# Causal pooling by running sums on VectorE in place of pooling-matrix products, and layer-norm moments and scaling of the gating branch at hooks of their own

## The chip, the cores and the metric

The kernel runs on one core of a Trainium2 chip. The metric is the device time of one execution in microseconds. Each of the core's engines (TensorE, or PE; VectorE, or DVE; ScalarE, or ACT; GpSimd, or POOL; SyncE, or SP) has a queue of instructions that it works off in order; they wait for each other through semaphores.

## The reference

Two transformer-like blocks on 256 tokens of width 2048, in fp32. Two places matter here. The first block has a spatial gating unit, whose second half `v` goes through a layer norm over its 1024 channels before it is mixed along the tokens:

```python
vn = layer_norm(v, ln_g, ln_b)
mixed = einsum('gqp,bnpgc->bnqgc', w_s, vn.reshape(...)) + b_s
y = u * mixed
```

The second block begins with a pool mixer. Its 4096 channels `u` are four groups of 1024; in group j each token gets the mean of the last w tokens (w = 2, 4, 8, 16, fewer at the beginning), less itself:

```python
z = xn @ w_in;  u, g = split(z, 2)
for j, w in enumerate((2, 4, 8, 16)):
    c = csum[:, :, group j]            # running sum over tokens, a zero ahead
    count = minimum(t + 1, w)
    pooled_j = (c[:, 1:] - lagged by w) / count - u[:, :, group j]
mixed = einsum('bsgc,gcd->bsgd', pooled, w_group)
out = (mixed * scale * silu(g)) @ w_out
```

## The kernel before

Nearly all the work is products with weights that pass through the core once. SyncE loads them as 1 MB units into four raw tiles. So that fp32 accuracy is reached with the faster fp32r products, each unit is split in two halves: ScalarE rounds a half (`w_hi`, line 1438), VectorE subtracts (`w_lo`, line 2036, counted by `lo_split`), and TensorE makes three products for each pair of operands (lines 829 to 831, or 913 to 916 where the result is wanted with channels on partitions). There are four buffers of halves: ScalarE rounds half h only when TensorE has left half h - 4 (`act.wait_ge(half_used, h - 3)`).

The work is cut into stages (`STREAM`, line 79 on), a stage into rounds and chunks; a chunk is 512 result columns. `pool_u` has 4 rounds of 2 chunks of 8 halves. A round of `pool_g` has chunks of 4, 8, 4 and 8 halves: a product of the pooled channels with `w_group`, then a gate. `in_h` has 2 rounds of 2 chunks of 8 halves, with one sum of the conditioning (`add_ada`, line 2064) behind each four halves. All other work of ScalarE and VectorE is put by hand between the halves, at hooks: `run` calls a hook in the middle of each chunk, `run_at` at given numbers of halves. What a hook does stands on its engine's queue ahead of the rounding or subtraction of the next half.

Pooling, before: VectorE scales a finished chunk into `u_stage`, tokens on partitions (`pool_u_out`, line 2608). Behind the next chunk TensorE multiplies it with a pooling matrix over the tokens (`pool_turn`, line 1194: 4 x 3 fp32 products, `k_pool` loaded by GpSimd), so that the pooled channels come out on partitions in PSUM. ScalarE rounds them to `pooled_hi` (`direct`, line 1472), VectorE subtracts to `pooled_lo` (`pool_rest`, line 2599) and frees the PSUM tile (`fm_empty`).

Elsewhere, as behind each chunk of `m1a`, a tile is only turned: `turn` (line 922) makes 8 transposes into the same PSUM tiles.

The gating branch, before: in `in_h`, VectorE's hook of the second chunk does `conv_sides(0)` and then the moments of both token tiles (`sgu_norm`, line 2266); ScalarE's of the third takes the root; VectorE's of the fourth does `conv_sides(2)` and then scales both tiles (`sgu_norm2`, line 2272).

## Time and profile before

| | us |
|---|---|
| median of 3 runs | 2746.13 |
| lowest, highest | 2746.08, 2747.34 |
| the profiled execution | 2747.47 |
| its span, first to last instruction | 2746.1 |
| TensorE busy | 2662.0 (97%) |
| VectorE busy | 1812.8 (66%) |
| ScalarE busy | 1274.3 (46%) |
| mean granted TensorE clock | 0.985 |

Products overlap, so starts tell more than durations: the distance from the start of one product to that of a later one is what the stretch cost. A row in brackets at the end of a timeline line tells how long the engine had stood idle and what released it. PEclk 1.00 is the 2.4 GHz level, 0.50 the 1.2 GHz level.

### The profile page before, as it was taken

Reading aid. Unit: us, or ns where it says so; the run is one execution under the profiler, and the core shown is the slowest. Engines: PE = TensorE matmul, PEld = TensorE weight load, DVE = VectorE, ACT = ScalarE, POOL = GpSimd, SP = SyncE. Lnnn points to the kernel's source line nnn. Section 1 sums busy time; section 2 is a strip of 40 time slices with the busy share of each in tenths; the row PEclk is TensorE's granted clock in tenths of the full one; section 3 lists DMA queues with packets and bytes.
Section 4 is the critical chain, followed back from the end, with each engine's and each line's share of the span. In section 5 each row is a group of like instructions: output and inputs, shape, how many; then the busy total and the mean of one; then the engine's idle time right before and its main releaser. Section 6 shows DMA issues by size and latency. Waiting matters only on the chain.

```text
span 2746.1 us, 31839 instructions
## 1 busy us (share of the span) xinstructions
PE 2662.0 (97%) x12702; PEld 2213.7 (81%) x12702; DVE 1812.8 (66%) x1869; ACT 1274.3 (46%) x1544; POOL 36.1 (1%) x58
## 2 busy tenths in 40 slices
PE   4899999999999999999999899999999999999999
PEld 2569998888878888888888788888888888888887
DVE  6877878877897654578766855555555565656565
ACT  1234444334344444565555433444444565555463
POOL 0000000000000000000000000000000000000000
PEclk8899999999999999999999999999999999999999
DMA  9987677878868865566555555555565555533654
GB/s 320 335 305 271 227 278 260 280 268 318 305 223 309 278 217 188 188 202 198 189 198 191 195 173 173 175 184 184 184 210 195 184 185 175 184 123 123 214 184 138
DMA packets 269205, 599.47 MB, mean 218 GB/s; under 512 B 12739, under 2 KB 13390, under 8 KB 258638
## 3 DMA queue, kind: packets, MB, share of 16 engines
q1 hardware_dynamic: 259680, 561.56, 60.5%
q0 software_dynamic: 5472, 26.25, 2.8%
q10 hardware_dynamic: 3918, 9.79, 1.0%
q8 instruction: 94, 1.54, 0.2%
q14 instruction: 41, 0.34, 0.0%
HBM read 587.07 MB, written 10.49 MB: 218 GB/s over the span
## 4 chain that ended last, share of the span: by engine, by line
PE 89%; DVE 7%; DMA 2%; issue 1%; ACT 1%; SPq 0%; DVEq 0%; ACTq 0%
PE ps L829 26%; PE ps L831 26%; PE ps L830 26%; DVE w_lo L2036 2%; PE ps L929 2%; PE ps L913 1%; PE ps L916 1%; PE ps L915 1%; DVE group_acc L2170 1%; DMA raw<-in_w_ada 1%; DMA raw<-in_w_in 1%; PE ps L1011 0%; PE ps L1003 0%; PE ps L1337 0%; PE ps L1338 0%
## 5 line engine op out<-in xcount | busy, mean ns | idle before, releaser
L2036 DVE TENSOR_TENSOR w_lo<-raw,w_hi 128x1024 fp32r<-128x1024 f32 x870 | 1050.2, 1221 | 737.4 <-ACT w_hi L1438 736.1
L1438 ACT CAST w_hi<-raw 128x1024 fp32r<-128x1024 f32 x870 | 906.6, 1051 | 1099.2 <-PE ps L831 968.1
L829 PE MATMUL ps<-w_lo,x_hi 128*128 128x512 f32 x2592 | 1019.0, 393 | 8.7 <-DVE w_lo L2036 4.9
L831 PE MATMUL ps<-w_hi,x_lo 128*128 128x512 f32 x2592 | 1011.3, 390 | 0.0
L830 PE MATMUL ps<-w_hi,x_hi 128*128 128x512 f32 x2592 | 1010.5, 390 | 0.0
L829 PEld LDWEIGHTS ps<-w_lo,x_hi 128*128 128x128 f32 x2592 | 488.1, 188 | 112.3 <-issue 7.4
L831 PEld LDWEIGHTS ps<-w_hi,x_lo 128*128 128x128 f32 x2592 | 487.5, 188 | 102.4
L830 PEld LDWEIGHTS ps<-w_hi,x_hi 128*128 128x128 f32 x2592 | 488.0, 188 | 99.8 <-issue 1.0
L829 PE MATMUL ps<-w_lo,pooled_hi 128*128 128x512 f32 x384 | 151.0, 393 | 2.5 <-DVE w_lo L2036 2.5
L2064 DVE SCALAR_TENSOR_TENSOR ada_acc<-raw,cond,ada_acc 128x2048 f32<-128x2048 f32 x64 | 150.0, 2344 | 0.3 <-DMA raw<-in_w_ada 0.3
L831 PE MATMUL ps<-w_hi,pooled_lo 128*128 128x512 f32 x384 | 149.5, 389 | 0.0
L830 PE MATMUL ps<-w_hi,pooled_hi 128*128 128x512 f32 x384 | 149.5, 389 | 0.0
L913 PE MATMUL ps<-x_hi,w_lo 128*128 128x256 f32 x384 | 110.0, 287 | 5.4 <-DVE w_lo L2036 5.4
L915 PE MATMUL ps<-x_hi,w_hi 128*128 128x256 f32 x384 | 109.6, 285 | 0.0
L916 PE MATMUL ps<-x_lo,w_hi 128*128 128x256 f32 x384 | 109.6, 285 | 0.0
L829 PEld LDWEIGHTS ps<-w_lo,pooled_hi 128*128 128x128 f32 x384 | 72.1, 188 | 19.8 <-DVE w_lo L2036 5.2
L831 PEld LDWEIGHTS ps<-w_hi,pooled_lo 128*128 128x128 f32 x384 | 72.1, 188 | 15.0
L2170 DVE SCALAR_TENSOR_TENSOR group_acc<-raw,cond,group_acc 128x1024 f32<-128x1024 f32 x60 | 77.0, 1283 | 10.9 <-DMA raw<-in_w_ada 8.4
L830 PEld LDWEIGHTS ps<-w_hi,pooled_hi 128*128 128x128 f32 x384 | 72.1, 188 | 14.6
L2559 DVE TENSOR_TENSOR x_lo<-ff,x_hi 128x1024 fp32r<-128x1024 f32 x64 | 77.9, 1217 | 7.4 <-ACT x_hi L1727 7.4
L913 PEld LDWEIGHTS ps<-x_hi,w_lo 128*128 128x128 f32 x384 | 74.8, 195 | 5.8 <-DVE w_lo L2036 5.8
L915 PEld LDWEIGHTS ps<-x_hi,w_hi 128*128 128x128 f32 x384 | 74.8, 195 | 0.0
(369 smaller groups left out, 2200.2 us busy)
## 6 DMA issues: line engine op xcount, KB each, us to landing
raw<-in_w_m SPq DMA_DIRECT2D x128, 1024.0 KB, 5.1
raw<-in_w_in SPq DMA_DIRECT2D x72, 1024.0 KB, 5.9
raw<-in_w_ada SPq DMA_DIRECT2D x64, 1024.0 KB, 5.0
raw<-in_pool_w_in SPq DMA_DIRECT2D x64, 1024.0 KB, 5.2
raw<-in_w_ada SPq DMA_DIRECT2D x64, 512.0 KB, 6.0
raw<-in_pool_w_out SPq DMA_DIRECT2D x32, 1024.0 KB, 5.1
raw<-in_ple_w_gate SPq DMA_DIRECT2D x32, 1024.0 KB, 5.1
raw<-in_mla_w_in SPq DMA_DIRECT2D x24, 1024.0 KB, 5.1
```

The costliest lines, as they stand in the source:

```text
L829: mm(bank, xh, wl, start=start, stop=False)
L830: mm(bank, xh, wh, start=False, stop=False)
L831: ins = mm(bank, xl, wh, start=False, stop=stop)
L913: mm(to, wl, x_hi[:, k, :], start=k == 0 and ct % 2 == 0, stop=False, skip_group_check=True)
L915: mm(to, wh, x_hi[:, k, :], start=False, stop=False, skip_group_check=True)
L916: ins = mm(to, wh, x_lo[:, k, :], start=False, stop=k == KT - 1, skip_group_check=True)
L929: ins = nc.tensor.transpose(fm_ps[slot][:, k, t * P:(t + 1) * P], src[:, t, (4 * q + k) * P:(4 * q + k + 1) * P], ident[:])
L1438: nc.scalar.copy(by_ktile(st, w_hi[st.half_slot(j, half)][:, 0:n]), raw_half(st, j, half)).then_inc(hi_split, 1)
L2036: tt(by_ktile(st, w_lo[slot][:, 0:n]), raw_half(st, j, half), by_ktile(st, w_hi[slot][:, 0:n].bitcast(F32)), ALU.subtract).then_inc(lo_spl ...
L2064: stt(out=buf[:], in0=raw[st.slot(j)][:], scalar=cond[:, ds(kk, 1)], in1=buf[:], op0=ALU.mult, op1=ALU.add).then_inc(ada_added, 1)
L2170: ins = stt(out=buf[:], in0=part, scalar=gain, in1=buf[:], op0=ALU.mult, op1=ALU.add)
L2559: tt(x_lo[:, s:s + 4], ff[:, 4 * u:4 * u + 4], x_hi[:, s:s + 4].bitcast(F32), ALU.subtract).then_inc(fm_lo, 1)
```

## The change

Pooling: TensorE only turns the chunk of `u` (`turn`, 8 transposes). ScalarE copies it from PSUM to `pool_src` and frees the PSUM tile (`pool_copy`). VectorE adds the tile to itself shifted by 1, 2, 4, 8 tokens, as many levels as the window wants (chunks 0 and 1 one, 2 and 3 two, 4 and 5 three, 6 and 7 four; `pool_levels`), then makes the mean and takes off `u` (`pool_mean`). ScalarE rounds the result (`pool_round`), VectorE subtracts (`pool_rest`). GpSimd loads 4 x 16 reciprocals in place of four 256 x 256 matrices. The gating: moments, scaling of tile 0 and scaling of tile 1 each get a hook of their own between other hooks of `in_h`.

```diff
         def pool_u_round(i):
             for c in range(2):
                 n = i * 2 + c
-                if n == 0:
-                    pe.wait_ge(pool_in, 16)
-                else:
+                if n > 0:
                     chunk(st, i, c, n + 50, c, x_hi, x_lo)
                     pe.wait_ge(pair_empty, n + 50)
-                    pool_turn(n + 35, i if c else i - 1, 1 - c)
+                    turn(n + 35, u_stage[1 - c], 0)
...
-            if n == 2:
+            if n == 1:
                 act.wait_ge(var_ready, 1)
                 nc.scalar.activation(rstd[:, 0], rstd[:, 0], ACT.Sqrt).then_inc(std_ready, 1)
...
+        def pool_copy(n):
+            act.wait_ge(fm_full, 37 + n)
+            nc.scalar.copy(pool_src[2 if n == 7 else n % 2][:], fm_ps[n % 2]).then_inc(fm_empty, 1)
+
+        def pool_round(n):
+            act.wait_ge(pooled, n + 1)
+            nc.scalar.copy(pooled_hi[:, 4 * n:4 * n + 4], pool_val[:]).then_inc(direct_hi, 1)
...
-            run(ST["pool_u"], i, pool_u_hook)
+            run_at(ST["pool_u"], i, {2: lambda: pool_u_hook(i, 0), 3: lambda: pool_copy(2 * i - 2), 10: lambda: pool_u_hook(i, 1),
+                                     11: lambda: pool_copy(2 * i - 1)})
...
         def pool_g_hook(i, c):
             if c == 0:
                 if i == 0:
-                    direct(42, pooled_hi[:, 24:28])
+                    pool_copy(6)
+                    pool_round(5)
                 else:
+                    if i == 1:
+                        pool_round(7)
...
+            if i == 0 and c == 1:
+                pool_copy(7)
             if c == 2:
+                if i == 0:
+                    pool_round(6)
                 pool_sigmoid(i, 0)
...
-        st = ST["in_h"]
-        for i in range(2):
-            run(st, i, in_h, lambda i, n: (2, 4 + 4 * i + n))
+        def sgu_scaled(t):
+
+            if t == 0:
+                dve.wait_ge(std_ready, 1)
+                then(nc.vector.reciprocal(rstd[:, 1], rstd[:, 0]))
+                dve.wait_ge(sgu_consts, 32)
+            v = vu[:, 0, t]
+            then(tsc(v, v, mv[:, t, 0:1], rstd[:, 1, t:t + 1], ALU.subtract, ALU.mult))
+            then(tt(v, v, sgu_g[:], ALU.mult))
+            tt(v, v, sgu_b[:], ALU.add).then_inc(vn_ready, 1)
+        run_at(ST["in_h"], 0, {4: lambda: vu_out(3), 8: sgu_norm, 12: lambda: conv_sides(0)}, lambda i, n: (2, 4 + n))
+        run_at(ST["in_h"], 1, {0: lambda: sgu_scaled(0), 4: lambda: conv_sides(1), 8: lambda: sgu_scaled(1),
+                               12: lambda: conv_sides(2)}, lambda i, n: (2, 8 + n))
...
         def pool_rest(n):
-            direct_rest(36 + n, DIRECT["pooled"] + n, pooled_hi[:, 4 * n:4 * n + 4], pooled_lo[:, 4 * n:4 * n + 4])
...
+            dve.wait_ge(direct_hi, DIRECT["pooled"] + n + 1)
+            then(tt(pooled_lo[:, 4 * n:4 * n + 4], pool_val[:], pooled_hi[:, 4 * n:4 * n + 4].bitcast(F32), ALU.subtract))
+
+        def pool_levels(n, levels):
+
+            if 0 in levels:
+                dve.wait_ge(fm_empty, 37 + n)
+            top = n // 2
+            for level in levels:
+                if level <= top:
+                    d, to = 1 << level, (pool_val, pool_sum)[(top - level + 1) % 2]
+                    src = pool_src[2 if n == 7 else n % 2][:] if level == 0 else (pool_sum, pool_val)[(top - level + 1) % 2][:]
+                    nc.vector.tensor_copy(to[:, :, 0:d], src[:, :, 0:d])
+                    then(tt(to[:, :, d:S], src[:, :, d:S], src[:, :, 0:S - d], ALU.add))
+
+        def pool_mean(n):
+
+            u, w = pool_src[2 if n == 7 else n % 2], WINDOWS[n // 2]
+            if n == 0:
+                dve.wait_ge(pool_in, 16)
+            head = pool_sum[:, :, 0:w - 1]
+            then(tt(head, head, pool_r[:, n // 2:n // 2 + 1, 0:w - 1].to_broadcast([P, 4, w - 1]), ALU.mult))
+            tt(pool_val[:, :, 0:w - 1], head, u[:, :, 0:w - 1], ALU.subtract)
+            stt(out=pool_val[:, :, w - 1:S], in0=pool_sum[:, :, w - 1:S], scalar=1.0 / w, in1=u[:, :, w - 1:S],
+                op0=ALU.mult, op1=ALU.subtract).then_inc(pooled, 1)
+
+        def pool_u_hooks(i):
+            hooks = {}
+            for c in range(2):
+                n, b = i * 2 + c, 8 * c
+                if n >= 3:
+                    hooks[b + 3] = lambda n=n: pool_rest(n - 3)
+                hooks[b + 4] = lambda n=n: (pool_u_out(n - 1), pool_levels(n - 2, (0, 1)))
+                hooks[b + 5] = lambda n=n: pool_levels(n - 2, (2, 3))
+                hooks[b + 6] = lambda n=n: pool_mean(n - 2)
+            return hooks
...
             if c == 0:
                 if i == 0:
                     pool_u_out(7)
-                    pool_rest(6)
+                    pool_rest(5)
+                    pool_levels(6, (0, 1))
                 else:
+                    if i == 1:
+                        pool_rest(7)
                     pool_product(i - 1, 1)
                     scaled_rest(i - 1, 0)
...
                 if i == 0:
-                    pool_rest(7)
+                    pool_levels(6, (2, 3))
+                    pool_mean(6)
             if c == 2:
+                if i == 0:
+                    pool_rest(6)
                 pool_product(i, 0)
+                if i == 0:
+                    pool_levels(7, (0, 1))
                 if i:
                     scaled_rest(i - 1, 1)
             if c == 3:
                 copy_pair(st, i, 2, 0, group_out[:])
+                if i == 0:
+                    pool_levels(7, (2, 3))
+                    pool_mean(7)
```

## Rows read from the trace of the kernel before

**Rows 1.** page, part 1: busy us (share of the span), instructions of each engine
```profile
PE 2662.0 (97%) x12702; PEld 2213.7 (81%) x12702; DVE 1812.8 (66%) x1869; ACT 1274.3 (46%) x1544; POOL 36.1 (1%) x58
```

**Rows 2.** waits of TensorE, whole span: waiter <- releaser: us, times, longest us
```profile
PE ps L829 <- DVE w_lo L2036: 8.4, 13, 1.6
PE ps L913 <- DVE w_lo L2036: 5.4, 2, 4.4
```

**Rows 3.** timeline, TensorE in in_h: start, duration, what [idle before <-releaser]
```profile
307.36 0.28 PE L916 MATMUL ps<-x_lo,w_hi 128*128 128x256 f32 x1
312.07 0.58 PE L913 MATMUL ps<-x_hi,w_lo 128*128 128x256 f32 x1 [4.43 <-DVE w_lo L2036]
...
317.05 0.28 PE L916 MATMUL ps<-x_lo,w_hi 128*128 128x256 f32 x1
```

**Rows 4.** timeline of TensorE, stage in_h, its first gap
```profile
260.09 0.28 PE L916 MATMUL ps<-x_lo,w_hi 128*128 128x256 f32 x1
...
261.53 0.28 PE L915 MATMUL ps<-x_hi,w_hi 128*128 128x256 f32 x1
```

**Rows 5.** timeline of VectorE in stage in_h
```profile
253.55 3.38 DVE L2242 SCALAR_TENSOR_TENSOR hy<-z_fm,fm_c,hy 128x255 f32<-128x255 f32 x8
256.84 1.28 DVE L2262 BATCH_NORM_STATS2 stats<-vu 128x6 f32<-128x512 f32 x2
...
260.04 4.62 DVE L2036 TENSOR_TENSOR w_lo<-raw,w_hi 128x1024 fp32r<-128x1024 f32 x4
...
286.87 2.34 DVE L2064 SCALAR_TENSOR_TENSOR ada_acc<-raw,cond,ada_acc 128x2048 f32<-128x2048 f32 x1
289.13 1.22 DVE L2036 TENSOR_TENSOR w_lo<-raw,w_hi 128x1024 fp32r<-128x1024 f32 x1
...
304.12 0.15 DVE L2274 RECIPROCAL rstd<-rstd 128x2 f32<-128x2 f32 x1
```

**Rows 6.** timeline of ScalarE in stage in_h
```profile
273.12 1.05 ACT L1438 CAST w_hi<-raw 128x1024 fp32r<-128x1024 f32 x1 [1.78 <-PE ps L916]
...
277.77 1.28 ACT L1619 ACT_TABLE_LOAD   x1
...
296.16 1.05 ACT L1438 CAST w_hi<-raw 128x1024 fp32r<-128x1024 f32 x1 [1.78 <-PE ps L916]
```

**Rows 7.** timeline of TensorE around the pooling products of one chunk
```profile
1579.53 0.39 PE L831 MATMUL ps<-w_hi,x_lo 128*128 128x512 f32 x1
...
1582.67 0.40 PE L830 MATMUL ps<-w_hi,x_hi 128*128 128x512 f32 x1
```

**Rows 8.** timeline of TensorE around a turn of one chunk, stage m1a
```profile
848.27 0.39 PE L831 MATMUL ps<-w_hi,x_lo 128*128 128x512 f32 x1
...
849.61 0.40 PE L830 MATMUL ps<-w_hi,x_hi 128*128 128x512 f32 x1
```

**Rows 9.** timeline, pool_u: a two-element VectorE instruction, a PSUM copy of ScalarE
```profile
1566.90 0.16 DVE L2650 RECIPROCAL rms<-rms 128x2 f32<-128x2 f32 x1
...
1582.64 1.02 ACT L1477 CAST pooled_hi<-ps 128x1024 fp32r<-128x1024 f32 x1 [1.63 <-PE ps L1204]
```

**Rows 10.** timeline of VectorE at the first hook of pool_g
```profile
1726.68 1.41 DVE L2614 TENSOR_SCALAR u_stage<-ps,rms 128x512 f32<-128x512 f32 x2 [3.13 <-PE ps L831]
```

**Rows 11.** timelines of TensorE and VectorE at the third chunk of pool_g
```profile
1764.51 0.39 PE L829 MATMUL ps<-w_lo,pooled_hi 128*128 128x512 f32 x1
...
1769.95 0.42 PE L829 MATMUL ps<-w_lo,pooled_hi 128*128 128x512 f32 x1
...
1768.59 4.62 DVE L2036 TENSOR_TENSOR w_lo<-raw,w_hi 128x1024 fp32r<-128x1024 f32 x4
```

**Rows 12.** stretches: us, busy by engine, PEclk, DMA share, GB/s; then two idle gaps
```profile
312.00:316.00 4.00, 3.93 (x18) 3.93 (x19) 4.00 (x5) 0.00 (x0) 0.00 (x0) 0.50 0.37 105
...
795.82 3.68 PE L929 MATMUL ps<-ident,res 128*128 128x128 f32 x16 [2.01 <-DVE res L2479]
...
1270.79 0.47 PE L829 MATMUL ps<-w_lo,x_hi 128*128 128x512 f32 x1 [1.57 <-DVE w_lo L2036]
```

More of the change, by code:

```diff
@@ L61, in tables @@
     window = np.exp(-lin * deltas)
-    pool = np.zeros((4, S, S))
-    for j, width in enumerate((2, 4, 8, 16)):
-        for to in range(S):
-            n = min(to + 1, width)
-            pool[j, to - n + 1:to + 1, to] = 1.0 / n
-            pool[j, to, to] -= 1.0
+    pool = np.stack([1.0 / np.minimum(np.arange(16) + 1, width) for width in WINDOWS])
     freq = (10000.0 ** (-np.arange(0, ROPE, 2, dtype=np.float32) / ROPE))[None, :]
@@ L250, in block_kernel @@
     pooled_lo = at("pooled_lo", 144, [E_POOL // P, S], F32R)
-    pool_m = at("pool_m", 180, [4, 2, S])
+    pool_r = at("pool_r", 188, [4, 16])
+    pool_sum = at("pool_sum", 190, [4, S])
+    pool_val = at("pool_val", 194, [4, S])
+    pool_src = [at(f"pool_src{i}", kb, [4, S]) for i, kb in enumerate((180, 184, 198))]
     u_stage = [at("u_stage0", 198, [2, CH]), at("u_stage1", 176, [2, CH])]
@@ L1192, in _ @@
         turned_chunk(st, 50, 32, lambda q: turn_normed(32, q, 4), x_hi, x_lo)
-        def pool_turn(g, n_group, c):
-            pe.wait_ge(fm_empty, g - 1)
-            slot = (g % 2) if isinstance(g, int) else c
-            u = u_stage[c]
-            for k in range(4):
-                f = slice(k * P, (k + 1) * P)
-                m = pool_m[:, ds(n_group, 1)].rearrange("p a t s -> p (a t) s")
-                mm(fm_ps[slot][:, k, 0:P], u[:, 0, f], m[:, 0, 0:P], start=True, stop=True)
-                mm(fm_ps[slot][:, k, P:S], u[:, 0, f], m[:, 0, P:S], start=True, stop=False)
-                ins = mm(fm_ps[slot][:, k, P:S], u[:, 1, f], m[:, 1, P:S], start=False, stop=True)
-            ins.then_inc(fm_full, 1)
         def pool_u_round(i):
@@ L1227, in pool_g_round @@
                         pe.wait_ge(pair_empty, 58)
-                        pool_turn(43, 3, 1)
+                        turn(43, u_stage[1], 0)
                 else:
@@ L1746, in pool_u_hook @@
             n = i * 2 + c
-            if n >= 2:
-                direct(36 + n - 2, pooled_hi[:, 4 * (n - 2):4 * (n - 1)])
+            if n >= 3:
+                pool_round(n - 3)
+        def pool_copy(n):
[4 more added lines that the diff above has]
+            nc.scalar.copy(pooled_hi[:, 4 * n:4 * n + 4], pool_val[:]).then_inc(direct_hi, 1)
         def pool_start():
@@ L2270, in sgu_norm @@
             tsc(rstd[:, 0], mv[:, :, 1], LN_EPS, None, ALU.add).then_inc(var_ready, 1)
-        def sgu_norm2():
-            dve.wait_ge(std_ready, 1)
-            then(nc.vector.reciprocal(rstd[:, 1], rstd[:, 0]))
-            dve.wait_ge(sgu_consts, 32)
-            for t in range(2):
-                v = vu[:, 0, t]
-                then(tsc(v, v, mv[:, t, 0:1], rstd[:, 1, t:t + 1], ALU.subtract, ALU.mult))
-                then(tt(v, v, sgu_g[:], ALU.mult))
-                tt(v, v, sgu_b[:], ALU.add).then_inc(vn_ready, 1)
-        def in_h(i, c):
-            n = 2 * i + c
-            if n == 0:
-                vu_out(3)
-            else:
-                conv_sides(n - 1)
-            if n == 1:
-                sgu_norm()
-            if n == 3:
-                sgu_norm2()
-        st = ST["in_h"]
-        for i in range(2):
-            run(st, i, in_h, lambda i, n: (2, 4 + 4 * i + n))
+        def sgu_scaled(t):
[10 more added lines that the diff above has]
+                               12: lambda: conv_sides(2)}, lambda i, n: (2, 8 + n))
         def sgu_gate():
@@ L2599, in pool_rest @@
         def pool_rest(n):
-            direct_rest(36 + n, DIRECT["pooled"] + n, pooled_hi[:, 4 * n:4 * n + 4], pooled_lo[:, 4 * n:4 * n + 4])
-        def pool_u_hook(i, c):
-            st = ST["pool_u"]
-            n = i * 2 + c
-            pool_u_out(n - 1)
-            pool_rest(n - 2)
+            dve.wait_ge(direct_hi, DIRECT["pooled"] + n + 1)
[23 more added lines that the diff above has]
+                n, b = i * 2 + c, 8 * c
+                if n >= 3:
+                    hooks[b + 3] = lambda n=n: pool_rest(n - 3)
[3 more added lines that the diff above has]
+            return hooks
         def pool_u_out(n):
@@ L2666, in _ @@
         for i in range(1, 4):
-            run(ST["pool_u"], i, pool_u_hook)
+            run_at(ST["pool_u"], i, pool_u_hooks(i))
         def scaled_rest(i, c):
```

7 lines of the change are left out of this document (4 added, 3 removed).

## The prediction

> **What bounds the kernel now.** I read the page's busy table first: TensorE is busy 97% of the span, VectorE 66%, ScalarE 46% [rows 1]. So time can be won only by taking work off TensorE's queue or by closing its gaps, and VectorE has room on average. Next the waits of TensorE [rows 2]: in all of the span it waits for VectorE's `w_lo` in 13 short gaps of 8.4 us at the 512-column products, and in two gaps of 5.4 us at line 913, the products of stage `in_h`. Line 913 is what the second half of the change touches. The timelines then give the unit in which I count. A half of a weight load (one `w_hi`/`w_lo` pair) is 24 products of 512 columns: 24 starts from 1764.51 to 1769.95, so 5.44 us are two halves and one half is 2.72 us [rows 11]. In `in_h` a chunk of eight halves takes 296.16 - 273.12 = 23.04 us, or 2.88 us a half [rows 6]. There are four buffers of halves: ScalarE may round a half once TensorE has left the half four earlier, and VectorE subtracts after it. At the end of a chunk three halves are therefore ready, and whatever VectorE does at a hook must be over, with the next subtraction of 1.22 us behind it, before TensorE arrives. This lead, and not VectorE's mean load, decides everything below.
>
> I call T the moment at which TensorE finishes one chunk.
>
> **Part 1, TensorE's own saving.** Pooling of one chunk is 12 fp32 products, 24 passes. From the last product ahead of it (start 1579.53) to the second one behind it (1582.67) are 3.14 us [rows 7]. The same kind of interval around a turn of a chunk, 8 transposes, is 849.61 - 848.27 = 1.34 us [rows 8]; the new `turn(n + 35, ...)` is this very function on a tile of the same shape. Saving 1.80 us a chunk, eight chunks: **14.4 us**, all of it on the path, since TensorE doesn't idle in these stretches. A turn without what surrounds it delays the next products by 1.34 - 2 x 0.23 = 0.88 us.
>
> **Part 2, `in_h`.** Gap one: 24 products should take 24 x 0.12 = 2.88 us, but from 307.36 to 317.05 they take 9.69 us [rows 3], so 6.8 us are lost. Of these 4.4 us are the wait; the rest is that the granted clock was 0.50 from 312 to 316 (the 1.2 GHz level) after the gap [rows 12]. Gap two: two steps take 261.53 - 260.09 = 1.44 us in place of 0.24 [rows 4], 1.2 us lost. The cause in both is a clump on VectorE: `conv_sides` of 3.38 us, then behind the first one the moments (256.84 to 260.04, 3.2 us), behind the third the scaling of both token tiles, which starts at 304.12 and lasts until about 310.8, one subtraction ahead of TensorE's restart at 312.07 [rows 3, 5]. The change puts 3.2 us (moments), 3.4 us (scale tile 0) and 3.3 us (scale tile 1) each at a hook of its own, eight halves or four halves from the next `conv_sides`. Is there room? At the hooks between chunks (8 of round 0, 0 and 8 of round 1) the next subtraction now starts at 289.13, which is 16.2 us behind T = 272.96 (0.16 ahead of ScalarE's row at 273.12) [rows 5, 6]. With 3.4 us ahead of it it ends at T + 20.8, and TensorE wants it at T + 23.0: 2.2 us to spare. With `conv_sides` alone the subtraction behind it starts 3.2 us earlier than 260.04 and is over at 258.1, while TensorE runs dry at 260.2: 2.1 us to spare [rows 4, 5]. The square root on ScalarE moves one chunk earlier; there, with its table load of 1.28 us [rows 6], it lies behind `conv_center` (over at T + 4.8) and puts the rounding of half 4 off to T + 7.3, which VectorE takes up at T + 8.2. Both gaps close: **8.0 us**. If a clump were late after all, the late part would come back one for one; bounds 0 and 8.0, and I take 8.0, as the two spare times agree.
>
> **Part 3, the new work on VectorE and ScalarE in `pool_u`.** No row shows a running-sum level, so I bound it. The add reads two fp32 tiles of 128x1024 in SBUF like `w_lo` or `pooled_lo`, 1.22 us; shifted operands are no dearer, as `conv_sides` reads 255 shifted elements in 0.42 us (eight in 3.38 us), and from there to 1024 unshifted ones in 1.22 us is 1.04 ns an element, with nothing left over for the shift [rows 5]. The small copy of 4 to 32 elements lies between nothing and the 0.16 us of a 128x2 instruction [rows 9]; I take 0.16 with 0.08 us overlapped, plus 0.03 us for the wait on its own semaphore: **1.33 us a level**, bounds 1.2 and 1.5. Chunks 0 to 7 need 1, 1, 2, 2, 3, 3, 4, 4 levels, 20 in all, 27 us. The mean is two small instructions and one of 1.22 us, 1.5 us, eight times 12 us. ScalarE gets eight copies of 1.02 us more [rows 9]. Against VectorE's idle time of half of each chunk (its `w_lo` rows are 2.7 us apart) that is hidden on average; the place decides. Within chunk n, from T: the turn has ended at 1.07, ScalarE copies until 2.1 and rounds half 3 until 3.1; VectorE subtracts it (4.3), empties the pair as before (1.41 us [rows 10], 5.7), two levels (8.4), half 4 (9.6, wanted at 0.88 + 4 x 2.72 = 11.8), a third level and half 5 (12.1, wanted at 14.5), the mean and half 6 (14.8, wanted at 17.2). At least 2.1 us to spare at each: no wait in `pool_u`, **0 us**. Behind this wait on the copy stand the `w_lo` of halves 4 and on, and TensorE waits for those; the spare times are its cover, and a level would have to cost 2.4 us before any showed. The table of reciprocals (32 KB in place of 1 MB) moves nothing: ScalarE isn't waiting for weights there.
>
> **Part 4, the first round of `pool_g`.** Here the hooks come earlier in a chunk, behind only two halves, and the cover is thinner. (a) Hook at half 2: from T VectorE empties the pair (it starts 0.20 us behind T, which is 1726.48 now, and ends at 1.6) [rows 10]. The new `pool_rest(5)` must wait for ScalarE: `pool_copy(6)` ends at 2.09, then `pool_round(5)` at 3.05, so the subtraction of 1.23 us ends at 4.3; two levels end at 7.0; the subtraction for half 2 ends at 8.3. TensorE wants it at 0.88 + 5.44 = 6.3. A **new wait of 2.0 us**. (b) Hook at half 14: T = 1764.51. Today sigmoid and products let four subtractions begin at 1768.59, the first of them lands at 1769.8 and TensorE starts at 1769.95: it is just in time [rows 11]. The change puts two levels of chunk 7 (2.7 us) right in front: VectorE goes on to half 14 only at T + 6.8, and its products start at T + 8.05 in place of T + 5.44, a **new wait of 2.6 us**. The other hooks of that round (half 8: copy, two levels and mean, over at 9.0 behind T, wanted at 11.8; half 20 the same with 10.9) stay covered. With 0.1 us of restart for each: **4.8 us** given back. Bounds: 4.2 and 6.0 by the bounds of a level.
>
> The Trainium skill, VectorE: DVE Perf Modes, section The TRN2 errata, says that SBUF-source instructions pay a fixed extra latency each and that many small ones pay it every time; this speaks against the twenty small copies and the heads of the means. Its table would put the fixed term at 58 cycles, its text beneath at about 150; the 0.16 us row of a two-element instruction [rows 9] sides with the 150. By the table the waits of part 4 would be 0.4 us shorter.
>
> **Sum.** 14.4 + 8.0 - 4.8 = 17.6 us. The span of 2746.1 us becomes 2728.5; the profiled execution took 2747.5 us and would take 2729.9. The runs shown have the median 2746.13, within 0.1 us of the span, so the median becomes **2728.5 us**, 0.64% less.
>
> **The rivals.** R1: the new waits of part 4 also cost clock. For it: the idle time of 4.43 us was followed by about 4 us at 1.2 GHz, dearer by 2.2 us than the wait itself, and behind one of 2.01 us sixteen transposes took 3.68 us, twice their time at full clock; against: one of 1.57 us left the clock as it was [rows 12]. Waits of 1.9 and 2.5 us lie between. One drop costs about 2 us (products 0.43 us apart in place of 0.23 for 4 us): 2730.5, both 2732.5. The Trainium skill, TensorE: Matmul & The Clock Gate, section Why this matters for your kernels, warns that an idle gap in the middle of a kernel can send the engine back to the lower rate; the trace agrees for the gap of 4.43 us.
> R2: no wait arises in part 4, because the copies overlap more than I assume or ScalarE's two steps come earlier: 2746.1 - 22.4 = 2723.7. Against it stands that half 14 has no spare time at all today, so at the very least the 2.6 us of (b) should show.
> R3: `in_h` keeps a part of its gaps, as VectorE's hooks with the condition sums (2.34 us every four halves [rows 5]) leave less than 2.1 us: one gap of up to 4 us with its clock, 2732 to 2735.
> R4, slower than before: a level is much dearer than an add of its size, because input and output tiles are read shifted and each level depends on the one before. Above 2.4 us a level every chunk from 2 to 5 stalls by 2 x level - 4.9 us, and both waits of part 4 grow by two levels' excess. At 4.0 us a level that is 4 x 3.1 + 7.3 + 7.9 = 27.7 us against 22.4: 2751. It passes the time of before at about 3.6 us a level. Against it: chained in-place instructions in `in_h` follow each other within 0.03 us, and shifted ones run at full rate.
> R5: the running sums save nothing because the turns take as long as the products did (if transposes ran as two passes too): 8 transposes in two passes would be 1.8 us, saving 0.9 us a chunk; 2735.6. The turns of `ff_stage` are fp32 as well, and show one pass.
>
> **How the numbers follow.** Forecast as summed, with none or one drop of the clock (2727 to 2731): 0.60. Both drops or a dearer level (R1, to 2735): 0.12. R2: 0.12. R3: 0.07. R5: 0.02. R4: 0.04, of which most is slower. The rest, 0.03, is for what I don't see. About 0.2%, 5.5 us, is the smallest difference that a measurement of this kernel can tell from none; forecast, R1, R2, R3 and R5 all lie beyond it on the faster side: 0.91. Within it 0.05, slower 0.04. The range of 8 in 10 takes in R2's 2723.7 below with 1.7 us for the turns' share, and above R3 and two drops: 2722 to 2735.
>
> **What would show it.** Eight groups of eight transposes from `u_stage`, each 1.03 us long, and no lines 1202 to 1204. TensorE's waits at the `in_h` products gone and the granted clock 1.00 from 225 to 320. In `pool_u` no wait for `w_lo` beyond those of the first chunk. Two waits of about 2 and 2.5 us some 6 us into the first chunk and 5 us into the third chunk of `pool_g`; if the granted clock there is below 1, R1 holds. VectorE's adds of the levels at 1.2 us. Wrong would make me: levels well over 1.5 us, a new wait in `pool_u`, or a late subtraction behind a hook of `in_h`.

## The result and the profile after

| | before | after |
|---|---|---|
| median, us | 2746.11 (4 runs) | 2727.39 (4 runs) |
| lowest, highest | 2745.34, 2747.34 | 2726.03, 2731.82 |
| the profiled execution | 2747.47 | 2727.24 |
| its span | 2746.1 | 2725.9 |
| mean granted TensorE clock | 0.985 | 0.987 |

The ratio of the times is 0.9936, with a 95% interval of 0.9924 to 0.9949: faster by 18.7 us. The forecast was 2728.5 us. In the changed kernel the lines of the products are one number higher (830 to 832, and 914 to 917 in `in_h`), and the turn stands in line 930.

The busy table of the page of after, to be read beside [rows 1]:

```profile
PE 2645.5 (97%) x12574; PEld 2195.6 (81%) x12574; DVE 1846.9 (68%) x1933; ACT 1281.7 (47%) x1552; POOL 35.9 (1%) x58
```

TensorE has 128 instructions less (8 x 24 products out, 8 x 8 transposes in), VectorE 64 more (20 levels of two, eight means of three). ScalarE has the eight copies more. TensorE stays the bound.

The waits of TensorE for VectorE's `w_lo` in after (us in total, times, longest us), against [rows 2]:

```profile
PE ps L830 <- DVE w_lo L2036: 12.8, 15, 2.5
```

There is no row for line 914 any more: the 5.4 us of `in_h` are gone. At the 512-column products there are two waits more, and 4.4 us more.

The stage `in_h`. First the rows of its first product's line, of before and of after (count, durations, first and last start), then the window 225 to 318 us of each (us, busy by engine, PEclk, DMA share, GB/s):

```profile
L913 PE MATMUL ps<-x_hi,w_lo x384: 278/283/581, 225.7 to 375.1; 128*128 128x256 f32 x192
225.00:318.00 93.00, 87.62 (x708) 87.10 (x707) 73.41 (x77) 43.53 (x57) 0.00 (x0) 0.96 0.72 250
```

```profile
L914 PE MATMUL ps<-x_hi,w_lo x384: 278/283/363, 222.9 to 364.3; 128*128 128x256 f32 x192
225.00:318.00 93.00, 93.00 (x779) 93.00 (x778) 76.99 (x81) 47.85 (x64) 0.00 (x0) 1.00 0.79 272
```

From first to last start the stage took 375.1 - 225.7 = 149.4 us and takes 364.3 - 222.9 = 141.4 us. In after TensorE is busy for all of the 93 us, at PEclk 1.00: both gaps of [rows 3, 4] and the stretch at 1.2 GHz behind the second are gone. VectorE's timeline of after shows the moments and the scaling of tile 0 away from `conv_sides` (start, duration, what; the moments begin at 240.62, `conv_sides` at 250.77, the scaling at 262.11):

```profile
240.62 1.29 DVE L2262 BATCH_NORM_STATS2 stats<-vu 128x6 f32<-128x512 f32 x2
...
250.77 3.38 DVE L2242 SCALAR_TENSOR_TENSOR hy<-z_fm,fm_c,hy 128x255 f32<-128x255 f32 x8
254.06 3.49 DVE L2036 TENSOR_TENSOR w_lo<-raw,w_hi 128x1024 fp32r<-128x1024 f32 x3
...
262.11 0.16 DVE L2276 RECIPROCAL rstd<-rstd 128x2 f32<-128x2 f32 x1
```

In [rows 5] four subtractions stood together behind the first clump, the sign of a full backlog; here never more than three do.

`pool_u`: TensorE at the turn of the first chunk, and the line of all its turns:

```profile
1567.04 0.40 PE L832 MATMUL ps<-w_hi,x_lo 128*128 128x512 f32 x1
1567.27 1.04 PE L930 MATMUL ps<-ident,u_stage 128*128 128x128 f32 x8
...
1568.38 0.39 PE L831 MATMUL ps<-w_hi,x_hi 128*128 128x512 f32 x1
```

```profile
L930 PE MATMUL ps<-ident,u_stage x64: 270/273/273, 1567.3 to 1717.9; 128*128 128x128 f32 x64
```

1568.38 - 1567.04 = 1.34 us, where [rows 7] has 3.14. VectorE at the levels of chunk 3, two levels and the mean:

```profile
1618.21 0.16 DVE L2602 COPY pool_val<-pool_src 128x4 f32<-128x4 f32 x1
1618.28 1.21 DVE L2603 TENSOR_TENSOR pool_val<-pool_src 128x1020 f32<-128x1020 f32 x1
1619.53 0.17 DVE L2602 COPY pool_sum<-pool_val 128x8 f32<-128x8 f32 x1
...
1620.86 2.36 DVE L2036 TENSOR_TENSOR w_lo<-raw,w_hi 128x1024 fp32r<-128x1024 f32 x2
1623.13 0.17 DVE L2611 TENSOR_TENSOR pool_sum<-pool_sum,pool_r 128x12 f32<-128x12 f32 x1
1623.33 0.17 DVE L2612 TENSOR_TENSOR pool_val<-pool_sum,pool_src 128x12 f32<-128x12 f32 x1
1623.42 1.21 DVE L2613 SCALAR_TENSOR_TENSOR pool_val<-pool_sum,pool_src 128x1012 f32<-128x1012 f32 x1
```

Two levels last from 1618.21 to 1620.86: 1.33 us each. TensorE has no wait in `pool_u` that it hadn't before.

The first of the two new waits of `pool_g`, before half 2, on TensorE, ScalarE and VectorE:

```profile
1709.42 0.39 PE L832 MATMUL ps<-w_hi,pooled_lo 128*128 128x512 f32 x1
1711.55 0.50 PE L830 MATMUL ps<-w_lo,pooled_hi 128*128 128x512 f32 x1 [1.74 <-DVE w_lo L2036]
1711.88 0.40 PE L831 MATMUL ps<-w_hi,pooled_hi 128*128 128x512 f32 x1
```

```profile
1704.37 1.01 ACT L1738 COPY pool_src<-ps 128x1024 f32<-128x1024 f32 x1 [5.27 <-PE ps L930]
1705.28 1.05 ACT L1742 CAST pooled_hi<-pool_val 128x1024 fp32r<-128x1024 f32 x1
```

```profile
1703.49 1.41 DVE L2633 TENSOR_SCALAR u_stage<-ps,rms 128x512 f32<-128x512 f32 x2 [3.14 <-PE ps L832]
1706.36 1.22 DVE L2591 TENSOR_TENSOR pooled_lo<-pool_val,pooled_hi 128x1024 fp32r<-128x1024 f32 x1 [1.46 <-ACT pooled_hi L1742]
...
1710.27 4.63 DVE L2036 TENSOR_TENSOR w_lo<-raw,w_hi 128x1024 fp32r<-128x1024 f32 x4
```

VectorE stands idle for 1.46 us until ScalarE has rounded, then does the subtraction and two levels, and four subtractions of weights have piled up behind (`x4`). Two steps of TensorE take 1711.88 - 1709.42 = 2.46 us in place of 0.45: 2.0 us lost. The second wait, before half 14:

```profile
1745.01 0.39 PE L832 MATMUL ps<-w_hi,pooled_lo 128*128 128x512 f32 x1
1747.90 0.72 PE L830 MATMUL ps<-w_lo,pooled_hi 128*128 128x512 f32 x1 [2.50 <-DVE w_lo L2036]
...
1752.12 0.40 PE L832 MATMUL ps<-w_hi,pooled_lo 128*128 128x512 f32 x1
```

```profile
1708.00:1712.00 4.00, 2.26 (x10) 1.56 (x10) 3.93 (x5) 2.21 (x3) 0.00 (x0) 1.00 0.00 0
1712.00:1716.00 4.00, 4.00 (x19) 3.27 (x18) 2.90 (x3) 1.04 (x1) 0.00 (x0) 1.00 0.53 155
...
1748.00:1752.00 4.00, 4.00 (x11) 3.13 (x12) 3.25 (x3) 0.00 (x0) 0.00 (x0) 0.57 0.44 131
```

Twelve steps take 1752.12 - 1745.01 = 7.11 us in place of 2.72: 4.4 us lost, 2.7 of them by the late `w_lo` (1747.90 in place of 1745.24) and 1.7 because the products behind it start 0.43 us apart. The windows (columns as above) say why: around and behind the wait of 1.74 us PEclk stays 1.00, behind that of 2.50 us it is 0.57.

Where did the time go? Two landmarks which both kernels have on TensorE's timeline, a product that waits ahead of the pooling of the first chunk and one that waits in round 1 of `pool_g`; first before, then after:

```profile
1563.31 0.50 PE L829 MATMUL ps<-w_lo,x_hi 128*128 128x512 f32 x1 [1.25 <-DVE w_lo L2036]
...
1804.14 0.50 PE L829 MATMUL ps<-w_lo,pooled_hi 128*128 128x512 f32 x1 [0.41 <-DVE w_lo L2036]
```

```profile
1550.77 0.50 PE L830 MATMUL ps<-w_lo,x_hi 128*128 128x512 f32 x1 [1.25 <-DVE w_lo L2036]
...
1783.84 0.50 PE L830 MATMUL ps<-w_lo,pooled_hi 128*128 128x512 f32 x1 [0.48 <-DVE w_lo L2036]
```

| stretch | before, us | after, us | change |
|---|---|---|---|
| start to first product of `in_h` | 225.7 | 222.9 | -2.8 |
| `in_h` | 149.4 | 141.4 | -8.0 |
| pooling: between the landmarks | 240.8 | 233.1 | -7.8 |
| all else | 2130.2 | 2128.5 | -1.7 |
| span | 2746.1 | 2725.9 | -20.2 |

The first and the last stretch are work that the change doesn't touch. The 1.7 us of the last lie almost wholly in one place, some 17 us behind `in_h`, where the same work ran at different clocks; before, then after:

```profile
392.00:396.00 4.00, 4.00 (x16) 3.35 (x14) 2.42 (x3) 1.02 (x1) 2.30 (x2) 0.57 1.03 414
```

```profile
381.00:385.00 4.00, 4.00 (x23) 3.42 (x23) 2.65 (x3) 1.27 (x2) 2.23 (x2) 1.00 1.04 401
```

So in the two profiled executions 15.8 us lie in what the change touches, and 4.5 us elsewhere (the sum is 20.2 by the unrounded starts). The medians differ by 18.7. The 2.8 us can't come from the change, as the two kernels are the same up to there. Of the dip in the clock behind `in_h` that isn't as sure: in the profiles of all kernels below it is there in the three kernels that keep a gap in `in_h` (before among them), and in four of the ten profiles of kernels that have none. It comes and goes with one and the same program, so it is at least not the change alone; whether a gap ahead of it makes it likelier stays open.

### The profile page after: what moved, and what is told of

The parts are those of the page before. It is cut to its first block, busy times and chain, and to the rows that moved or that the text cites. A ratio compares the mean times of both kernels' runs of the same rounds, so it can differ in the third digit from the quotient of the medians.

```text
span 2725.9 us, 31673 instructions
## 1 busy us (share of the span) xinstructions
PE 2645.5 (97%) x12574; PEld 2195.6 (81%) x12574; DVE 1846.9 (68%) x1933; ACT 1281.7 (47%) x1552; POOL 35.9 (1%) x58
## 4 chain that ended last, share of the span: by engine, by line
PE 90%; DVE 6%; DMA 2%; issue 1%; ACT 1%; SPq 0%; DVEq 0%; ACTq 0%
PE ps L830 26%; PE ps L832 26%; PE ps L831 26%; PE ps L930 2%; PE ps L917 2%; PE ps L916 2%; PE ps L914 2%; DVE w_lo L2036 1%; DVE group_acc L2170 1%; DMA raw<-in_w_ada 1%; DMA raw<-in_w_in 1%; PE ps L997 0%; PE ps L1012 0%; PE ps L1004 0%; PE ps L1323 0%
```

## The experiments

The theory: 8.0 us come from the two gaps of `in_h`, 14.4 us from TensorE's shorter queue, and some 5 to 6.5 us are given back at two waits in the first round of `pool_g`, caused by the place of the levels and not by their number; the longer one costs clock too (R1). The rivals: the gain comes from elsewhere (the two parts don't add up), the waits aren't caused by the levels (R2 says they cost nothing), or VectorE's room in `pool_u` is smaller than reckoned, so that a level somewhat dearer would already lose (R4). Times are medians with lowest and highest; the ratio is to the kernel before on the same chip, which had medians of 2745.2 to 2746.1 us.

**Only the gating.** The kernel before, with the hooks of `in_h` as in the change (`sgu_scaled` and ScalarE's root one chunk earlier go with them):

```diff
...
-        st = ST["in_h"]
-        for i in range(2):
-            run(st, i, in_h, lambda i, n: (2, 4 + 4 * i + n))
+        run_at(ST["in_h"], 0, {4: lambda: vu_out(3), 8: sgu_norm, 12: lambda: conv_sides(0)}, lambda i, n: (2, 4 + n))
+        run_at(ST["in_h"], 1, {0: lambda: sgu_scaled(0), 4: lambda: conv_sides(1), 8: lambda: sgu_scaled(1),
+                               12: lambda: conv_sides(2)}, lambda i, n: (2, 8 + n))
```

> The kernel before with the gating half of the change alone. Theory (lead of three halves, one clump at a time): both waits at line 913 go, granted clock 1.00 from 225 to 318, 8.0 us faster than before, 2738.1. Rival (the time between the hooks of in_h was already all used, so that the late part comes back at another hook): a wait of 1 to 4 us stays at line 913 and less than 5 us are gained. Second rival (the unexplained 4.4 us of the full change belong to the gating half): 12 us faster, 2734.

Measured 2736.74 us (2734.26 to 2739.22), ratio 0.9966 (0.9952 to 0.998): 9.4 us less. Its products of `in_h` go from 224.9 to 366.3, 141.4 us, as in after, and no wait stands at their line.

**Only the pooling.** The changed kernel with the gating as before:

```diff
...
-        run_at(ST["in_h"], 0, {4: lambda: vu_out(3), 8: sgu_norm, 12: lambda: conv_sides(0)}, lambda i, n: (2, 4 + n))
-        run_at(ST["in_h"], 1, {0: lambda: sgu_scaled(0), 4: lambda: conv_sides(1), 8: lambda: sgu_scaled(1),
-                               12: lambda: conv_sides(2)}, lambda i, n: (2, 8 + n))
+        st = ST["in_h"]
+        for i in range(2):
+            run(st, i, in_h, lambda i, n: (2, 4 + 4 * i + n))
```

> The changed kernel with the gating branch as before. Theory: 14.4 us saved by turns in place of products, 2.0 and 2.6 us given back by the two waits in the first round of pool_g and 1.8 us by the 1.2 GHz stretch behind the second: 8.0 us faster than before, 2738.1; both waits at line 913 (now 914) are there as before. Rival (the drop of the clock at the second wait is chance): between 8.0 and 9.8 us faster from run to run. Second rival (the unexplained 4.4 us belong to the pooling half): 12 us faster.

Measured 2737.84 us (2735.97 to 2740.61), ratio 0.9972 (0.9963 to 0.9981): 8.3 us less. The waits of `in_h` are back (5.4 us in two, 149.3 us for the stage), and the two of `pool_g` are the same as in after, 1.73 and 2.49 us. The two halves bring 9.4 + 8.3 = 17.7 us, both together 18.7. Within the 1 us that medians here can tell they add up, and neither leans on the other.

**The levels spread.** In the first round of `pool_g` each step of VectorE gets a hook of its own:

```diff
+        run_at(ST["pool_g"], 0, {2: lambda: (pool_copy(6), pool_round(5)), 8: lambda: pool_copy(7),
+                                 10: lambda: pool_round(6), 14: lambda: pool_sigmoid(0, 0)})
...
+        run_at(ST["pool_g"], 0, {
+            2: lambda: pool_u_out(7), 3: lambda: pool_rest(5), 4: lambda: pool_levels(6, (0, 1)),
+            6: lambda: pool_levels(6, (2, 3)), 8: first_group_copy, 9: lambda: pool_mean(6), 11: lambda: pool_rest(6),
+            12: lambda: pool_levels(7, (0, 1)), 13: lambda: pool_levels(7, (2, 3)), 14: lambda: pool_product(0, 0),
+            20: lambda: copy_pair(ST["pool_g"], 0, 2, 0, group_out[:]), 21: lambda: pool_mean(7)})
```

> The changed kernel with VectorE's work of the first round of pool_g spread over more hooks: rest of chunk 5 at half 3, levels of chunk 6 at halves 4 and 6, its mean at half 9 and its rest at half 11, levels of chunk 7 at halves 12 and 13, mean at half 21; ScalarE's rounding of chunk 6 at half 10. Theory (what counts is how much stands ahead of one subtraction, not the sum): both waits of 1.74 and 2.50 us go, and with them the 1.2 GHz stretch, 6.4 us faster than the changed kernel, 2721.0. Rival (VectorE's mean load in this round is the limit): the waits come back at other halves and under 2 us are gained.

Measured 2722.38 us (2720.06 to 2725.16), ratio 0.9919 (0.9905 to 0.9933). Both waits are gone. TensorE's waits for `w_lo`:

```profile
PE ps L830 <- DVE w_lo L2038: 8.5, 13, 1.6
```

These are the 8.4 us in 13 of [rows 2] again. From the first turn of `u_stage` to the first of `pool_stage` it takes 203.2 us, in after 209.6 (1567.27 to 1776.84): 6.4 us less, the 2.0 and 4.4 us that I read off at the two waits. All the work is still there, so its place made the waits. At the first wait more than the levels moved: the subtraction of chunk 5, which waits for ScalarE, stands one half later too. The interval of the ratio overlaps that of after, so it is the trace that shows the gain. I call the distance between those turns the pooling stretch below.

**One level before the wait.** Only level 0 of chunk 7 stays in front of half 14, three go to the next hook:

```diff
-                    pool_levels(7, (0, 1))
+                    pool_levels(7, (0,))
...
-                    pool_levels(7, (2, 3))
+                    pool_levels(7, (1, 2, 3))
```

> The changed kernel with one level of chunk 7 instead of two in front of half 14 of the first round of pool_g, the other moved to half 20. Theory: the wait there becomes 1.3 us shorter (2.50 to about 1.2), and such a wait leaves the clock at 2.4 GHz, so the 1.8 us behind it go too: 3.1 us faster than the changed kernel, 2724.3; half 20 stays on time (ready at 10.3 us behind the chunk's start, wanted at 10.9). Rival (the clock falls after any wait here): 1.3 us faster only. Second rival (half 20 has less room than I count): a new wait in front of half 20.

In the trace it is as expected. The wait is one level shorter, and the clock stays up behind it:

```profile
1752.49 0.50 PE L830 MATMUL ps<-w_lo,pooled_hi 128*128 128x512 f32 x1 [1.17 <-DVE w_lo L2036]
```

```profile
1752.00:1756.00 4.00, 3.51 (x15) 2.90 (x16) 3.84 (x4) 0.76 (x2) 0.00 (x0) 1.00 0.29 69
```

The stretch takes 206.7 us, 2.9 less than after: 1.3 us of wait and 1.6 of clock. But the median was 2728.0 us (2725.72 to 2730.19), ratio 0.9933 (0.992 to 0.9947), no lower than after's. That called for the next runs.

**After once more,** the changed kernel itself, unchanged.

> The changed kernel itself, once more. The profile of it ran 4.4 us shorter ahead of and behind stage in_h than the steps of the prediction say: 2.8 us in stage first and 1.6 us behind the one-column products of ada_sum. Theory (these are the granted clock's luck, in work that the change doesn't touch): another execution of the same kernel has other values there, the start of in_h scatters over 2 to 3 us between profiles, and the median lies at 2727 to 2731. Rival (the change moved something ahead of in_h): the start of in_h is at 222.9 us again.

Measured 2725.93 us (2723.55 to 2729.76), ratio 0.9938 (0.9924 to 0.9951). The pooling stretch is again 209.6 us, the waits 1.77 and 2.50 us, and the second again costs clock. This is a property of the program, not of one execution. The first product of `in_h` starts at 221.5 us, where the profile of after had 222.9: that start does scatter with one program. The median is 1 us below the 2727 to 2731 that I had expected.

**One level, once more.**

> The kernel with one level of chunk 7 in front of half 14 once more. In its trace the stretch from the first transposes of u_stage to the first of pool_stage was 206.7 us, 2.8 us less than in the changed kernel, but its median, 2728.0, was no lower. Theory (the start of in_h, 225.5 us there and 222.9 in the changed kernel, is luck and hid it): a median of 2723 to 2726 now, between the spread and the changed kernel. Rival (something outside this stretch got slower by the edit): 2727 or more again, and a start of in_h above 225 again.

Measured 2726.01 us (2723.38 to 2727.6), ratio 0.9926 (0.9912 to 0.994); stretch 206.7 us as before, start of `in_h` 224.7. The two ratios of this kernel, 0.9933 and 0.9926, are 0.0003 and 0.0010 below the lower of after's two (0.9936), some 1 to 3 us, and the intervals overlap. So the median lies where the theory has it, but doesn't decide between theory and rival. What the trace shows to a tenth of a microsecond the median can't: outside the stretch the profiled spans were 2516.4 and 2515.0 us (after, twice), and 2522.2 and 2518.1 us (this kernel, twice), for the same work. The first of this kernel's profiles has the dip in the clock behind `in_h` (PEclk 0.50 in one window of 4 us), the second hasn't.

**The clump put back.** To see whether it is the place of the scaling or the order as a whole that closes the gaps: moments moved as in the change, both scalings again behind `conv_sides(2)`:

```diff
-        run_at(ST["in_h"], 1, {0: lambda: sgu_scaled(0), 4: lambda: conv_sides(1), 8: lambda: sgu_scaled(1),
-                               12: lambda: conv_sides(2)}, lambda i, n: (2, 8 + n))
+        run_at(ST["in_h"], 1, {4: lambda: conv_sides(1), 12: lambda: (conv_sides(2), sgu_scaled(0), sgu_scaled(1))},
+               lambda i, n: (2, 8 + n))
```

> The changed kernel, but both scalings of the gating tiles stand in one clump behind conv_sides of the fourth chunk of in_h, as before; the moments stay at their new hook. Theory: the first wait (1.2 us lost) stays closed, the second is back with 4.4 us of wait and 2.4 us of half clock: 6.8 us slower than the changed kernel, 2734.2. Rival (the first gap was the cause of the second): under 3 us slower.

Measured 2737.74 us (2734.44 to 2740.69), ratio 0.9973 (0.9962 to 0.9983). One wait is back, and with it the slow clock:

```profile
PE ps L914 <- DVE w_lo L2036: 4.4, 1, 4.4
```

```profile
312.00:316.00 4.00, 4.00 (x20) 4.00 (x20) 4.00 (x4) 0.00 (x0) 0.00 (x0) 0.50 0.48 147
```

The stage takes 148.9 us, 7.5 more than in after (expected 6.8; the slow stretch behind the gap has 28 products here, 22 in before), while the first gap stays closed. Each clump makes its own gap. The median is 10 to 12 us above after's, of which the trace explains 7.5 in the stage, and some 1.6 more by the dip in the clock behind `in_h`, which this profile has too.

**Each level's add twice, then three times** (the same sum is written again, so only VectorE's time grows):

```diff
-                    then(tt(to[:, :, d:S], src[:, :, d:S], src[:, :, 0:S - d], ALU.add))
+                    for _ in range(2):
+                        then(tt(to[:, :, d:S], src[:, :, d:S], src[:, :, 0:S - d], ALU.add))
```

> The changed kernel with each level's large add done twice (same result), a level of 2.6 us in place of 1.33. Theory: in pool_u the spare 2.1 us in front of half 4 are used up to the last 0.3 us for chunks with two levels or more, so waits of 0.3 us at most, four of them; the two waits of pool_g grow by 2.5 us each, to 4.2 and 5.0, with half clock behind both: 8 to 10 us slower than the changed kernel. Rival (VectorE's mean load limits): 20 adds of 1.25 us come through, 25 us slower.

> The changed kernel with each level's large add done three times (same result), a level of 3.8 us. Theory (a level dearer than 2.4 us stalls each of the chunks 4 to 7 of pool_u by twice the level less 4.9 us): four waits of about 2.7 us in front of half 4 in pool_u, more where a third level stands in front of half 5, and the two waits of pool_g at 7 and 7.5 us: 20 to 27 us slower than the changed kernel, which is about the time of the kernel before. Rival (mean load): 40 adds of 1.25 us come through, 50 us slower.

Twice: 2740.05 us (2736.05 to 2743.81), ratio 0.9984 (0.9975 to 0.9993); the pooling stretch is 220.4 us, 10.9 more than after, and the median is 13 to 14 us above after's two (expected 8 to 10). Two levels now take 5.1 us. On TensorE a start at half 4 of the third chunk, then the waits that are new or grown up to half 14:

```profile
1625.38 0.39 PE L832 MATMUL ps<-w_hi,x_lo 128*128 128x512 f32 x1
1625.83 0.50 PE L830 MATMUL ps<-w_lo,x_hi 128*128 128x512 f32 x1
...
1675.66 0.50 PE L830 MATMUL ps<-w_lo,x_hi 128*128 128x512 f32 x1 [0.64 <-DVE w_lo L2036]
...
1718.74 0.79 PE L830 MATMUL ps<-w_lo,pooled_hi 128*128 128x512 f32 x1 [4.24 <-DVE w_lo L2036]
...
1759.12 0.80 PE L830 MATMUL ps<-w_lo,pooled_hi 128*128 128x512 f32 x1 [5.00 <-DVE w_lo L2036]
```

At half 4 the list of waits has no row, but the starts do: 0.45 us from 1625.38 to 1625.83 in place of 0.23, so the product is 0.22 us late, and in the three other chunks with two levels or more it is 0.23 to 0.26 us. The formula's answer was 2 x 2.57 - 4.9 = 0.2 us. A wait of 0.64 us and one of 0.66 stand at half 5 of the two chunks with a third level, where my expectation had none. The prediction's own count has them: half 5 ready at 12.1 + 3 x 1.24 = 15.8 us behind T and wanted at 14.5, some 0.4 us later still by what half 4 lost; 0.8 us late is what the starts show. The waits of the two hooks of `pool_g`, (a) and (b) in the prediction, grow by 2.5 us each, that is two more adds, and now (a) costs clock too.

Three times: 2767.77 us (2763.84 to 2772.02), ratio 1.0082 (1.0065 to 1.01), slower than before by 22 us. Two levels take 7.65 us (3.83 each), and the formula gives 2 x 3.83 - 4.9 = 2.8 us for the chunks 2 to 5:

```profile
1627.07 0.39 PE L832 MATMUL ps<-w_hi,x_lo 128*128 128x512 f32 x1
1630.03 0.50 PE L830 MATMUL ps<-w_lo,x_hi 128*128 128x512 f32 x1 [2.57 <-DVE w_lo L2036]
...
1631.31 0.63 PE L832 MATMUL ps<-w_hi,x_lo 128*128 128x512 f32 x1
1631.74 0.63 PE L830 MATMUL ps<-w_lo,x_hi 128*128 128x512 f32 x1
```

The product starts 2.96 us behind the last one in place of 0.23: 2.7 us late, four times over (2.57, 2.60, 2.57, 2.59 us of idle time). So the room in `pool_u` is what I reckoned, and a level of 1.33 us is well within it. The size, though, was missed: I had expected 20 to 27 us above after, and it is 40. The trace has 41.1 us more in the stretch. Of these 26.1 are idle time (38.9 us of waits for `w_lo` in place of 12.8), among them 1.92 and 2.82 us at the hooks of halves 8 and 20, which I had called covered for a level of 1.33 us. The other 15 us are the clock and the restarts: eight gaps are followed by slow products, where after has one, most of them 1.7 us dearer by it and the two longest some 2.6, and each gap makes the next product 0.16 us later than its idle time says (2.73 for 2.57).

**A version that beats both.** On top of the spread levels, in the rounds 1 to 3 of `pool_g` the subtraction behind the gate (`scaled_rest`) moves one half back:

```diff
-                scaled_rest(i - 1, 0)
...
+            return {2: first, 3: lambda: scaled_rest(i - 1, 0), 8: lambda: copy_pair(ST["pool_g"], i, 0, 0, group_out[:]),
+                    14: lambda: pool_product(i, 0), 15: lambda: scaled_rest(i - 1, 1),
+                    20: lambda: copy_pair(ST["pool_g"], i, 2, 0, group_out[:])}
```

> The spread kernel, and in the rounds 1 to 3 of pool_g VectorE's scaled_rest stands one half later (half 3 and half 15 in place of 2 and 14), behind the subtraction that TensorE wants first. Theory (the same lead decides there): the six waits of 0.40 to 0.51 us in front of halves 2 and 14 go, with 0.1 us of restart each: 3.3 us faster than the spread kernel. Rival (the work only comes late at the next half): as many waits at halves 3 and 15, no gain.

> The spread kernel once more, on the chip of the other two, since single medians of five runs scatter by some 3 us. Theory: from the first transposes of u_stage to the first of pool_stage 203.2 us as before (209.5 in the changed kernel), and a median of 2720 to 2723. Rival: the shorter stretch is given back behind it, and the median is that of the changed kernel, 2726 to 2728.

Measured 2717.93 us (2714.9 to 2720.55), ratio 0.9897 (0.9881 to 0.9912), beside 2722.03 us (2717.12 to 2724.88), ratio 0.9909 (0.9894 to 0.9924), for the spread levels alone on the same chip. The waits for `w_lo` that are left:

```profile
PE ps L830 <- DVE w_lo L2038: 6.0, 7, 1.6
```

The intervals of the two overlap, so here too the gain rests on the trace. Six waits of 0.41 to 0.48 us are gone. From the first to the last turn of `pool_stage` it takes 213.9 us (1774.3 to 1988.2) in place of 218.3 (1774.6 to 1992.9): 4.4 us for 2.5 us of waits, as each gap also slowed the products behind it a little. One of the six, in the spread kernel, with the product ahead of it and two behind:

```profile
1780.70 0.39 PE L832 MATMUL ps<-w_hi,pooled_lo 128*128 128x512 f32 x1
1781.57 0.50 PE L830 MATMUL ps<-w_lo,pooled_hi 128*128 128x512 f32 x1 [0.48 <-DVE w_lo L2038]
1781.91 0.40 PE L831 MATMUL ps<-w_hi,pooled_hi 128*128 128x512 f32 x1
```

The step to it costs 0.87 us in place of 0.23, and the next 0.34: 0.75 us for a gap that the view calls 0.48.

## Why the prediction was right, and where it was off

*Part 1, 14.4 us: right.* The turn in `pool_u` is the turn of `m1a`, to the hundredth: 1.34 us against [rows 8]. With 14.4 us off and 2.0 and 4.4 us back, the stretch between the landmarks should be 8.0 us shorter; it is 7.8. One step of the text is wrong and harmless: a half is 12 products of 512 columns, not 24. The 24 starts in 5.44 us are two halves, and the 2.72 us of a half, with which all went on, are right.

*Part 2, 8.0 us: right.* 149.4 to 141.4 us. The gating alone brings the same 8.0 us in the trace; the clump put back takes 7.5 of it away.

*Part 3, 0 us: right, and for the stated reason.* A level costs 1.33 us, as summed from the add of 1.21 and a small copy of which 0.08 us counts. Twice and three times the adds gave the lateness of the formula to a tenth of a microsecond (0.22 for 0.2, 2.73 for 2.8), so the room was really counted and not just large enough. R4's price was too coarse. R4 said that the time of before is passed at 3.6 us a level. The runs have 2740 us at 2.57 and 2768 us at 3.83 us a level; a straight line between them passes 2746 at about 2.9. R4 had left out the clock behind each wait, half 5, and the hooks at halves 8 and 20.

*Part 4, two new waits: right in place and length, short in price.* For (a), counted from T = 1703.29 (0.20 us ahead of VectorE's row at 1703.49, as in [rows 10]): ScalarE's copy ends at T + 2.09 (predicted 2.09), its rounding at T + 3.04 (3.05), VectorE's levels at T + 6.98 (7.0); TensorE loses 2.0 us (2.0 and 0.1). For (b) the wait makes TensorE 1747.90 - 1745.24 = 2.7 us late (2.6 and 0.1). The cause is shown too: spreading the same work removes both, one level less in front of (b) makes its wait 1.33 us shorter, and two adds more make each 2.5 us longer. The step that failed in size is the term of (b): 4.8 us were to be given back in all, 6.4 us are, because the clock falls behind the second wait. That is above the stated bounds of 4.2 and 6.0, which were to come from the price of a level alone (1.2 to 1.5 us a level in four places would have given 4.3 to 5.5). The drop is R1's, at one of the two waits. I had put that case inside the forecast's range with its own price of 2 us (measured 1.7), but not in the sum. With it the sum is 22.4 - 6.4 = 16.0 us, and 15.8 us is what the traces show for the parts that the change touches.

*The total.* 17.6 us forecast, 18.7 us by the medians. That the two are so near is partly luck: the mechanism gives 16.0, and the remaining 2 to 3 us lie in work that the change leaves alone (in the profiled pair 4.5 us, ahead of `in_h` and behind it). If the dip behind `in_h` is really likelier behind a gap, three of three against four of ten profiles at some 1.6 us each, then about 1 us of that would be the change's after all; this is an estimate, and no run decides it. Over all profiles (the work ahead of `in_h` is the same in each) its first product starts between 221.5 and 226.8 us; a forecast of this kernel can't be checked finer than that by its total.

*The rivals.* R1 came half true: one drop of the clock, not two. R2 (no wait in `pool_g`) fell: both waits are there, and the drop behind the second, in each of the four profiles that keep this order (after twice, only the pooling, the clump put back). R3 (`in_h` keeps a part) fell: no gap. R5 (turns in two passes) fell: 1.34 us. R4 fell at its premise, the price of a level. The rule of the Trainium skill, VectorE: DVE Perf Modes, section The TRN2 errata, was weighed in the prediction. The small copy lasts 0.16 to 0.18 us, which is with the 150 cycles of its text and not the 58 of its table. But what a small copy takes from the queue is less, since the add behind it starts 0.07 to 0.09 us later: the twenty of them cost 1.5 us of VectorE's time together, and it was right to count the overlap.

## What to carry to other kernels

Where an engine of preparation runs ahead of TensorE by a few buffers, count at each hook from the moment at which TensorE finishes a chunk: what stands on the queue before the next subtraction, and when TensorE wants it. A mean load of 66% said nothing of the two waits, while this count gave them within a tenth of a microsecond, and moving the same work by one or two halves was worth 6.4 and 4.4 us. A list of waits hides what is shorter than its threshold: the four delays of 0.22 to 0.26 us stood only in the starts. Price a gap by the distance of the starts around it, the slow products behind it included; here a gap of 2.5 us cost 4.4 and one of 0.48 us cost 0.75.

## What the runs showed of the hardware

*The clock behind an isolated gap.* In all of these cases TensorE waited for `w_lo`, and the products ahead of the gap had run at 2.4 GHz; gaps behind slow work are not among them. Behind idle times of 1.17, 1.25, 1.57 and 1.73 to 1.77 us the granted clock stayed at that level. Behind 1.92 us, 2.49 to 2.50, 2.57 to 2.60, 2.82, 4.24, 4.43, 5.00, 6.75 and 7.50 us it was at 1.2 GHz for a while. Up to 2.82 us that was mostly seven or eight products 0.43 us apart, 1.7 us lost; behind 6.75 and 7.50 us eleven of them, some 2.6 us. Behind 4.43 us, at products of 256 columns, it was 20 to 28 of them 0.21 us apart, 2.0 to 2.8 us lost. I had the drop behind 4.43 us in the rows of before and had left it open for 1.9 and 2.5 us; nothing here says why it is there behind 1.92 and not behind 1.77. It need not begin with the first product behind the gap: in the kernel with three adds the products at 1630.03 to 1631.07 still run at full pace, and those from 1631.31 on are slow. The Trainium skill, TensorE: Matmul & The Clock Gate, section Why this matters for your kernels, warns of idle gaps in the middle of a kernel. The traces agree, and show the drop behind shorter gaps too than the section names: 1.92 us was enough in one case.

*Small instructions on VectorE.* One of 4 to 32 elements lasts 0.16 to 0.19 us. If the next doesn't read its result, that one starts 0.07 to 0.11 us behind it (1618.21 to 1618.28, 1623.33 to 1623.42). If it does, the kernel has a semaphore wait between the two, and it is 0.19 to 0.21 us (1623.13 to 1623.33).

*Transposes.* Eight fp32 transposes of 128x128 put the products behind them off by 1.34 - 2 x 0.23 = 0.88 us, 0.11 us each. The Trainium skill, TensorE: Matmul & The Clock Gate, section Part 4: PE-mode transpose, gives about 275 ns for one of bf16 in a kernel's context; the fp32 ones here have rows of 270 to 273 ns. They overlap, though: eight together last 1.04 us. What the change saves in part 1 is their number: the 24 instructions of a pooling product start 0.11 us apart as well, so 16 fewer of them are the 1.80 us. The transposes didn't cost the clock either: TensorE stays at the pace of 2.4 GHz behind them (0.23 us from 1568.38 on).
